# Encoder layer, attention stage: GpSimd forms the low half of the probabilities, VectorE sums the exponentials in a PSUM bank

## The reference

```python
def attend(qb):
    scores = jnp.einsum('bqhd,bkhd->bhqk', qb, k, preferred_element_type=jnp.float32)
    p = jax.nn.softmax(scores, axis=-1).astype(v.dtype)
    return jnp.einsum('bhqk,bkhd->bqhd', p, v)
```

## Time and profile before

| | before |
|---|---|
| runs | 4531.1, 4539.14, 4552.52 us, median 4539.14 |
| span of the profiled execution | 4533.2 us |
| PE, PEld busy | 3947.0 (87%), 3175.3 (70%) |
| DVE, ACT, POOL busy | 2457.6 (54%), 1943.8 (43%), 1319.8 (29%) |
| POOL L1131, the additions | 684.5 us, 448 of them |
| DVE L1025, the low halves | 712.5 us, 640 of them |
| DVE L986, the reductions | 421.7 us, 640 of them |
| attention, first to last exponential | 599.0 to 2082.2 us of the span |

### The profile page before, as it was taken

One profiled execution on the slowest core, in us unless ns is written; L12 is line 12 of the kernel. 1 busy time (PEld: TensorE's weight loads), 2 busy tenths in 40 slices (PEclk: granted clock), 3 DMA queues, 4 the chain that ended last, 5 costly groups with the idle time before them and its releaser, 6 DMA issues. The chain is left out here.

```text
span 4533.2 us, 56177 instructions
## 1 busy us (share of the span) xinstructions
PE 3947.0 (87%) x19385; PEld 3175.3 (70%) x19385; DVE 2457.6 (54%) x3666; ACT 1943.8 (43%) x3429; POOL 1319.8 (29%) x906
## 2 busy tenths in 40 slices
PE   7799899999999987885799427999999999999992
PEld 1799656666666664653577317999999899999991
DVE  1322188888889895788322484444444444444443
ACT  0444256566666663653222104344433343434342
POOL 0000067777777783553211040000010100000000
PEclk9899888898989998997899758999999999999996
DMA  7222200000000001003444105445454454454536
GB/s 261 85 75 70 91 4 6 4 7 6 7 6 4 5 5 44 12 9 116 158 148 148 45 1 181 145 139 157 139 149 143 151 163 153 139 157 139 157 107 241
DMA packets 296383, 428.21 MB, mean 94 GB/s; under 512 B 43558, under 2 KB 206246, under 8 KB 295050
## 3 DMA queue, kind: packets, MB, share of 16 engines
q1 hardware_dynamic: 269900, 327.41, 22.1%
q0 software_dynamic: 13824, 50.34, 4.9%
q10 hardware_dynamic: 12480, 48.24, 2.7%
HBM read 335.88 MB, written 90.06 MB: 94 GB/s over the span
## 5 line engine op out<-in xcount | busy, mean ns | idle before, releaser
L1131 POOL TENSOR_TENSOR att_acc<-att_acc,att_e 128x512 f32<-128x512 f32 x448 | 684.5, 1542 | 308.6 <-ACT att_e L917 302.9
L1025 DVE TENSOR_TENSOR att_pr<-att_e,att_pr 128x512 fp32r<-128x512 f32 x640 | 712.5, 1115 | 82.1 <-ACT att_pr L923 79.8
L917 ACT ACTIVATE att_e<-att_s_ps 128x512 f32<-128x512 f32 x640 | 377.7, 590 | 362.2 <-PE att_s_ps L787 331.8
L1958 ACT ACTIVATE moe_wh<-moe_raw 128x1024 fp32r<-128x1024 f32 x384 | 374.0, 1045 | 311.6 <-DMA moe_raw<-w_up 188.9
L799 PE MATMUL att_o_ps<-att_pr,att_v 128*128 128x512 f32 x1280 | 442.6, 429 | 69.8 <-DVE att_pr L1025 57.9
L1879 POOL DMA_INDIRECT s_x<-moe_ye,moe_to_add x48 | 75.8, 1580 | 1441.3 <-issue 1152.9
L986 DVE TENSOR_REDUCE att_mx<-att_m_ps 128x1 f32<-128x512 f32 x640 | 421.7, 679 | 108.8 <-PE att_m_ps L726 106.4
L2005 DVE TENSOR_TENSOR moe_wl<-moe_raw,moe_wh 128x1024 fp32r<-128x1024 f32 x384 | 444.7, 1221 | 43.4 <-ACT moe_wh L1958 43.4
L923 ACT ACTIVATE att_pr<-att_e 128x512 fp32r<-128x512 f32 x640 | 402.3, 629 | 16.6 <-PE att_o_ps L799 1.6
L1915 PE MATMUL moe_a_ps<-moe_xh,moe_wh 128*128 128x384 f32 x1024 | 349.8, 342 | 46.0 <-DVE moe_hf L2033 42.9
L799 PEld LDWEIGHTS att_o_ps<-att_pr,att_v 128*128 128x128 f32 x1280 | 243.6, 201 | 169.6 <-DVE att_pr L1025 109.4
(11 more groups left out here) (238 smaller groups left out, 8187.3 us busy)
## 6 DMA issues: line engine op xcount, KB each, us to landing
moe_raw<-w_gate SPq DMA_DIRECT2D x64, 1024.0 KB, 5.3
moe_raw<-w_up SPq DMA_DIRECT2D x64, 1024.0 KB, 7.7
moe_raw<-w_down SPq DMA_DIRECT2D x64, 1024.0 KB, 6.4
ada_wa<-w_ada SPq DMA_DIRECT2D x12, 2048.0 KB, 10.2
s_x<-outp_x ACTq DMA_DIRECT2D x24, 512.0 KB, 5.5
s_xn<-outp_xn ACTq DMA_DIRECT2D x24, 512.0 KB, 6.4
fin_x<-s_x SPq DMA_DIRECT2D x12, 1024.0 KB, 12.0
inp_x<-x_sample SPq DMA_DIRECT2D x8, 1024.0 KB, 5.2
```

The costliest lines, as they stand in the source:

```text
L917: nc.scalar.activation(e[:, s % RING, :], s_ps[s % 2][:, :], ACT.Exp, scale=SCALE).then_inc(exp_done, 1)
L1025: nc.vector.tensor_tensor(pr[:, s % RING, 1, :], e[:, s % RING, :], pr[:, s % RING, 0, :].bitcast(F32), ALU.subtract).then_inc(lo_done, 1)
L1131: nc.gpsimd.tensor_tensor(acc[:, b % 2, kt % 2, :], acc[:, b % 2, kt % 2, :], e[:, s % RING, :], ALU.add).then_inc(sum_done, 1)
L1958: nc.scalar.activation(wh[:, s, part, :], raw[:, s, part, :], ACT.Copy).then_inc(w_hi_done, 1)
```

## The change

- `low` moves from VectorE to GpSimd: same instruction, same operands, 640 of them. On GpSimd it stands at the start of a step, ahead of the rotation's `q_sum`; `q_low` moves two steps behind `q_sum` (before, it followed at once).
- The 592 additions on GpSimd (448 of L1131, 96 of L1127, 48 of L1135) go. VectorE's `add_up` takes their place: at kt 0 a copy of `e` into a PSUM bank `acc_ps`, then additions of `e` in place in that bank, and at the block's last step an addition whose output is `acc` in SBUF. That is 640 instructions, one per step, where `low` stood. Each waits for the one before it.
- `acc` has one accumulator per block instead of two. The bank comes from the maxima's ring: MB = 2 instead of 3, which also holds for the value projection and the first units.
- The waits of ACT and PE on the sum (`sum_done`) count steps instead of additions.

```diff
-    MB = 3
+    MB = 2
...
-        acc = m.sb("acc", [P, 2, 2, BANK])
-        wv = acc[:, 0]
+        acc = m.sb("acc", [P, 2, BANK])
+        wv = acc[:]
...
+        acc_ps = m.ps("acc_ps")
...
-            def low(hp, s):
-                dve.wait_ge(hi_done, hp * PER + s + 1)
-                nc.vector.tensor_tensor(pr[:, s % RING, 1, :], e[:, s % RING, :],
-                                        pr[:, s % RING, 0, :].bitcast(F32), ALU.subtract).then_inc(lo_done, 1)
+            def add_up(hp, s):
+
+                b, kt = s // NT, s % NT
+                dve.wait_ge(exp_done, hp * PER + s + 1)
+                if from_start(hp, s - 1):
+                    dve.wait_ge(sum_done, hp * PER + s)
+                if kt == 0:
+                    step = nc.vector.tensor_copy(acc_ps[:, :], e[:, s % RING, :])
+                elif kt < NT - 1:
+                    step = nc.vector.tensor_tensor(acc_ps[:, :], acc_ps[:, :], e[:, s % RING, :], ALU.add)
+                else:
+                    if from_start(hp, b - 2):
+                        dve.wait_ge(den_ready, hp * NG + b - 1)
+                    step = nc.vector.tensor_tensor(acc[:, b % 2, :], acc_ps[:, :], e[:, s % RING, :], ALU.add)
+                step.then_inc(sum_done, 1)
...
                     if from_start(hp, s - 1):
-                        low(hp, s - 1)
+                        add_up(hp, s - 1)
...
+            def low(hp, s):
+                pool.wait_ge(hi_done, hp * PER + s + 1)
+                nc.gpsimd.tensor_tensor(pr[:, s % RING, 1, :], e[:, s % RING, :],
+                                        pr[:, s % RING, 0, :].bitcast(F32), ALU.subtract).then_inc(lo_done, 1)
+
             def body(hp, last):
-                split = NQB if from_start(hp, 0) and not from_start(hp, -1) else None
                 for s in range(PER):
-                    b, kt, h, j = at(s)
-
-
+                    if from_start(hp, s - 1):
+                        low(hp, s - 1)
                     qb = projecting(hp, s, QSPLIT - 1, last)
                     if qb is not None:
                         pool.wait_ge(q_shifted, hp * NG + NQB + qb + 1)
-                        pool.wait_ge(sum_done, (hp * NG + (s - 1) // NT) * SUMS + (SUMS if kt == 0 else summed(s - 1)))
+                        pool.wait_ge(q_lo_done, hp * NG + NQB + qb)
+                        pool.wait_ge(lo_done, hp * PER + s)
                         q_sum()
+                        pool.wait_ge(q_added, hp * NG + NQB + qb + 1)
+                    qb = projecting(hp, s, QSPLIT + 1, last)
+                    if qb is not None:
                         pool.wait_ge(q_hi_done, hp * NG + NQB + qb + 1)
                         q_low(1 - qb // NQB % 2, qb % NQB)
```

More of the change, by code:

```diff
@@ L542, in attention @@
     CT_PIECES = 4
-    SUMS = NT - 1
     WQ_IN = 3 * 16
@@ L647, in finish @@
                 do(hp, b)
-        def summed(s):
-            return (1, 1, 2, 2)[s % NT] if s % NT < 4 else s % NT - 1
         def projecting(hp, s, delay, last):
@@ L803, in denominators @@
             def denominators(hp, b):
-                pe.wait_ge(sum_done, (hp * NG + b + 1) * SUMS)
+                pe.wait_ge(sum_done, hp * PER + (b + 1) * NT)
                 pe.wait_ge(osum_done, hp * NG + b + 1)
                 for c in range(CB):
-                    mm = nc.tensor.matmul(o_ps[b % 2][:, c:c + 1], acc[:, b % 2, 0, c * P:(c + 1) * P], ones[:, :],
+                    mm = nc.tensor.matmul(o_ps[b % 2][:, c:c + 1], acc[:, b % 2, c * P:(c + 1) * P], ones[:, :],
                                           start=True, stop=True)
@@ L915, in exps @@
                     act.wait_ge(lo_done, hp * PER + old + 1)
-                    act.wait_ge(sum_done, (hp * NG + old // NT) * SUMS + summed(old))
+                    act.wait_ge(sum_done, hp * PER + old + 1)
                 nc.scalar.activation(e[:, s % RING, :], s_ps[s % 2][:, :], ACT.Exp, scale=SCALE).then_inc(exp_done, 1)
@@ L1077, in _ @@
             over_pairs(dve, body)
-            low(PAIRS, -1)
+            add_up(PAIRS, -1)
             for s in range(OUT + 1):
@@ L1113, in body @@
                         pool.wait_ge(q_shifted, hp * NG + NQB + qb + 1)
-                        pool.wait_ge(sum_done, (hp * NG + (s - 1) // NT) * SUMS + (SUMS if kt == 0 else summed(s - 1)))
+                        pool.wait_ge(q_lo_done, hp * NG + NQB + qb)
+                        pool.wait_ge(lo_done, hp * PER + s)
                         q_sum()
+                        pool.wait_ge(q_added, hp * NG + NQB + qb + 1)
+                    qb = projecting(hp, s, QSPLIT + 1, last)
+                    if qb is not None:
                         pool.wait_ge(q_hi_done, hp * NG + NQB + qb + 1)
                         q_low(1 - qb // NQB % 2, qb % NQB)
[L1118 to L1136, removed]
             over_pairs(pool, body)
+            low(PAIRS, -1)
 def pooling(nc, w, keep):
```

## The result

The changed kernel takes 4421.6 us (median of 4 runs, 4415.0 to 4425.4) against 4536.0 of the kernel before (4 runs): ratio 0.974, 95% interval 0.971 to 0.977. Forecast were 4408 us and faster; the range was 4340 to 4510. The profiled execution's span is 4413.2 us, 120 less than before.

A forecast was written before the change was run, and what follows sets the result against it. It took TensorE's values waiting for VectorE's low half as the bound. From the span, 4533.2 - 80 + 21 - 52 - 20 = 4402; the median lies 6 us above, so 4408 us, range 4340 to 4510.

The forecast's parts named there:

- The bound: In the attention TensorE's values wait for VectorE's low half; a long-sequence block with no wait would take 28.9 us.
- The low half's wait: TensorE's values wait 90 us for the low half; 10 us would be left in all 48 blocks: -80 us.
- The prices: Low half on GpSimd 1.29 us (bounds 1.26 and 1.58); VectorE's sum in PSUM 0.60 to 0.65 (bounds 0.60 and 1.20).
- GpSimd's slack of 1.7 us: Low half ends 2.7 us after its step's scores, its values come 4.4 us after them: 1.7 us to spare.
- The ring: Two maxima banks, not three: units wait 10 us in 25 blocks, 21 in seven value-split ones, less today's 10: +21 us.
- sign that the ring decides: Units in the attention waiting over 60 us on the reductions would show the forecast wrong.
- The clock: In the long sequence 77 us are lost to the lowered clock; 25 would be left: -52 us.
- The short sequence: In the short sequence: waits for the maxima -7, on the low half about -8, clock -5: -20 us.
- The value projection and the first units on two banks: Before the attention's scores, a bank is free long before it is needed: no cost; uncovered it would be 16 us.
- A slow sum: Rival: VectorE's sum in PSUM takes 1.20 us and TensorE stands at each unit: 4616 us, slower; chance 0.09.
- a slow GpSimd: Rival: GpSimd's low half takes 1.58 us, and 66 us of the 90 stay: 4505 us; chance 0.08.
- a clock that stays: Rival: short stops of TensorE at the two-bank ring keep the clock where it is: 4465 us; chance 0.12.

The follow-up runs named there:

- e6: The changed kernel with LAG = 2 instead of 3, values issued one TensorE step (1.4 us) earlier: 4498.2 us, ratio 0.991.
- e7: The changed kernel with q_low directly behind q_sum again, no low half between them: 4497.1 us, ratio 0.991.
- e10: The changed kernel with the low half kept on VectorE, so only the sum moves into PSUM: 4504.8 us, ratio 0.993.
- e4: The changed kernel with the four v_low of each head on GpSimd at the same steps: 4374.8 us, ratio 0.963.
- e8: The changed kernel with v_low left on VectorE and the long sequence's value split five steps later: 4379.5 us, ratio 0.965.
- e3: The changed kernel with VectorE's running sum in SBUF and three banks (MB = 3): 4530.9 us, ratio 0.998.
- e1: The kernel before with MB = 2 instead of 3 and nothing else: 4522.7 us, ratio 0.996.

## Why the prediction was right, and where it was off

**The bound.** Right. TensorE waited for the low half behind VectorE's stretched instructions; with that gone a plain block is 30.3 us, 1.4 over the 28.9 worked out for a block with no wait, where it was 34.9.

**The low half's wait, 90 us to 10.** Right: 86 us (2.78 x 31) to 10 (0.33 x 31).

**The prices.** The low half on GpSimd 1.29, the sum 0.69: at the nearest rows, `q_low` and L1032. Both unknown costs lay near the lower bound. VectorE was busy 760 us in a window of 1000 (740 forecast).

**GpSimd's slack of 1.7 us.** Right as to its edges: 1.4 us less (e6) or the rotation in one piece (e7) costs 77 and 76 us. The rule of the Trainium skill (GPSIMD Engine Reference, section 4.1) against elementwise work on GpSimd is right about the price, 1288 ns against VectorE's 673 in e10. It did not decide, since e10 to the changed kernel, the low half's move alone, gives 83 us.

**The ring, +21 us: mis-sized.** It came to +39 (0.32 to 1.59 us in 31 blocks). The 0.4 us of plain blocks are 0.5. The seven value-split blocks wait 5.5 us for units, not 3. The step that failed was the price of `v_low`: I kept the 901 ns of the earlier trace rows "still stretched by GpSimd", but GpSimd's list had changed, and with it what stands beside `v_low` behind the rotation. Where no `v_low` took over 1.51 us before, one in each of the seven now takes 3.4 to 5.2. That this instruction is the cause is shown twice, by e4, which takes it off VectorE, and by e8, which changes nothing but the place of the value split; the reason why VectorE is not let in is not shown. The prediction's own sign that the ring decides, over 60 us of units waiting, is met as the weight load sees it (69.4 us), and not by TensorE's matmuls (39.1, or 49 by the table).

**The clock, -52 us.** Right: 73 us to 24, and what is left is in the value-split blocks and the first block (0 in the plain ones).

**The short sequence, -20.** It came to -26.

**The value projection and the first units on two banks, at nothing: missed.** The first scores come 4 us later. From the first matmul of the value projection to these scores it is 72.2 us before and 71.7 in e3, with three banks, and 76.1 in the changed kernel, 75.0 in e1 and 74.0 to 76.8 in the ten others, with two. TensorE's matmuls wait 7.3 us for the copies there (`att_v_all`; 5.8 in e1) where it was 4.9 (5.2 in e3), and 2.4 for reductions (1.8 in e1) where it was 1.0. The rest of what the runs show is the start of the stage, which moves by up to 6 us between them.

**The sum of the terms.** In the long sequence the three terms give -76, +39 and -49, that is -86 of the -97; smaller waits and the last block give the rest. In all, the forecast's terms come to -131 against -120 measured: the ring took 18 us more than forecast and the missed term 4, and the short sequence, the smaller waits and the last block gave some of it back.

**The rivals.** A slow sum, a slow GpSimd and a clock that stays did not come. But e10 tests the price that I had put on the slow sum: it has the same 1.80 us a step of VectorE, in three instructions in place of two, and took 4505, where the rival said 4616. Its working added TensorE's waits and the lost clock to the block; in fact a block is little longer than the work of the engine that bounds it (33.2 us for 31.4), and waits in stops of at most 1.2 us cost 0.4 us of clock a block. By this run the slower side of the forecast was priced too high.

## What to carry to other kernels

Look at which instructions stretch each other before counting an engine's load: here one operand in PSUM instead of SBUF made the move of work worth 114 us, and with the sum in SBUF the same move was worth about 11 (e3). When work goes to another engine, look again at which instructions the two engines still stretch, and look for each one's longest duration, not its median: `v_low` five steps later gave 42 us more, and on GpSimd as well 63. A wait that is rare and long tells another story than one that is short and everywhere; the count and the longest in the waits' rows tell them apart.

## What the runs showed of the hardware

- An instruction of VectorE with two SBUF inputs does not just share with GpSimd or wait for one instruction of it: it lasted over four back-to-back ones (5.24 us for 0.4 us of work) and over five in e7 (6.6 us); elsewhere, as in e8, it got in between two of them. The Trainium skill (SBUF — State Buffer, section "Who interferes with whom") says that a VectorE instruction with two SBUF inputs contends with a GpSimd one that reads SBUF, and that the order of issue decides which of the two blocks. The trace agrees that they hold each other up, but the one shut out, issued 0.02 us behind a low half, was passed over by three more instructions of GpSimd.
- VectorE adding in place in a PSUM bank costs no more than reading it: 677/689/700 ns for 128x512, and 675/692/693 where the output is in SBUF. It is not stretched, and GpSimd's low half beside it stays at a median of 1287 ns; those of over 1.4 us run beside a `v_low`.
- The same 3.6 us of waiting in a plain block cost 2.4 us of clock with three banks and 0.7 with two (e1), where it was split into more and shorter stops (9.2 a block in place of 5.9). The Trainium skill (TensorE: Matmul & The Clock Gate, section "A second HAM failure mode") blames the clock's swings in one kernel on frequent micro-idles while it cycles through PSUM banks; here more of them went with a steadier clock, 0.95 against 0.93.
